# One stage of a hybrid sequence model: the S5 mixer by chunks of four tokens instead of token by token

## Chip, cores, metric

One core of a Trainium2 chip. The metric is the device time of one execution in microseconds; before the change three runs gave 3873.88, 3874.48 and 3877.62 us, a median of 3874.48 us.

## What is computed

A two-layer step over 256 prompt tokens and 8 samples of 4 tokens (288 tokens, width 2048): RMS norm, S5 mixer, a retrieval feed-forward over 16384 experts (PEER), then norm, RG-LRU mixer, PEER, final norm. The change touches the S5 mixer alone. Its reference, cut:

```python
bu_re = einsum("btgc,gpc->btgp", u, bb_re); bu_im = einsum("btgc,gpc->btgp", u, bb_im)   # 128 groups of 16 channels, 64 states
# the samples add a * h0 to their first token
s_re, s_im = scan over t of  s[t] = a * s[t-1] + bu[t]        # a complex, one per group and state
y = einsum("btgp,gcp->btgc", s_re, c_re) - einsum("btgp,gcp->btgc", s_im, c_im) + d_skip * h
y = gelu(y); out = y * sigmoid(y @ w_glu + b_glu)
```

The 128 x 64 = 8192 complex states are laid out as 64 columns ("state columns") of 128 partitions; four state columns belong to one tile of 128 channels, 16 tiles in all. The last states are outputs too.

## The kernel before, in words

Five engine programs run side by side and meet at semaphores; the order of the work is written out by hand. Line numbers are those of the profile.

Start: SyncE loads X (three tiles of 128 tokens, L321), then the S5 matrices B and C of a tile (L327, L333) and after them the first four GLU weight slabs (L344). VectorE and ScalarE work out the discrete parameters (L1373 to L1406, L1006 to L1015). The norm gives HN (L961, L963, L1342), TensorE turns it (L635), ScalarE copies it to HT (L978): channels on partitions, tokens along the free dimension.

S5 stage, 16 tiles: the complex recurrence is made real by rotation. In a tile of four state columns, TensorE multiplies B with the inputs (L735, L737), VectorE rotates 4 x 256 values by -phase * t with sine and cosine tables (L1425 to L1431), runs eight real scans of 256 tokens with the decay as factor (L1435), and rotates back by four products (L1441 to L1444). TensorE multiplies with C and D (L748, L754), ScalarE applies GELU into YT (L1036). The tables are made by ScalarE (L1021, L1022, sines at L1028 and L1032) with one VectorE step between (L1411). GpSimd scales B (L426 to L432), runs the samples' four steps one by one (L446 to L458) and writes the diagonal of D (L415).

After the stage, TensorE waits for all GELUs and makes the GLU product from YT (L648, 16 weight slabs of 1 MB, ring W of four slots), ScalarE the sigmoid (L1107), VectorE the gate (L1468). Then come the transposes back to token rows (L664), the second norm, the queries (L688) and, from about 620 us to the end, PEER and the LRU chain. None of that is changed, save that the gain row of the second norm is loaded later.

Two helpers matter for reading the code: `settle(ins)` on VectorE waits until its own last instruction has finished, `x.wait_ge(sem, n)` holds everything behind it on that engine.

## Time and profile before

| what | value |
|---|---|
| span of the profiled execution | 3880.3 us |
| time of the profiled execution | 3882.19 us |
| median of the three runs | 3874.48 us |
| busy: TensorE, VectorE, ScalarE, GpSimd | 59%, 75%, 12%, 38% of the span |
| chain that ended last | DMA 51%, DVE 26%, PE 16%, issue 6% |
| HBM traffic | 1404.75 MB, mean 362 GB/s |

Busy shares are means over stages with different limits: the PEER stages move expert rows at 410 to 428 GB/s, while the S5 stage, the first eleventh of the span, moves almost nothing. PE is a matmul, PEld its weight load, DVE is VectorE, ACT ScalarE, POOL GpSimd, SP SyncE. PEclk is the granted TensorE clock as a share of 2.4 GHz, 0.5 being 1.2 GHz. In a timeline row of several instructions the length runs from the first start to the last end; from one row's start to the next one's is what an instruction costs when the engine has work lined up (its "step"), and it is shorter than the listed duration, since the end of one overlaps the next.

### The profile page before, as it was taken

How to read it: one execution, taken by the hardware profiler on the slowest of the kernel's cores; microseconds unless marked ns; L12 is line 12 of the kernel's file. 1: busy time of each engine (PE TensorE's matmuls, PEld its weight loads, DVE VectorE, ACT ScalarE, POOL GpSimd, SP SyncE). 2: the span in 40 equal slices, each digit the busy share in tenths (PEclk: the TensorE clock that was granted, in tenths of full speed). 3: DMA queues.
4: the chain of work that ended last, by engine and by line, in shares of the span. 5: the costliest groups of instructions: out<-in, count | busy, mean ns of one | idle time of the engine just before them, and what ended most of it. 6: DMA issues, size and time to landing. Idle time of an engine off the chain costs nothing.

```text
span 3880.3 us, 30905 instructions
## 1 busy us (share of the span) xinstructions
PE 2277.3 (59%) x9698; PEld 1387.9 (36%) x9698; DVE 2899.6 (75%) x4162; ACT 456.3 (12%) x901; POOL 1471.3 (38%) x1739
## 2 busy tenths in 40 slices
PE   5667996000087777659499876470189773003776
PEld 2334775000022227559275346460056321001222
DVE  7995048999966568896768777868958768998655
ACT  6662121000000002220000012200000000000000
POOL 4885005434343333222323342223433434334332
PEclk8878998555599999779799988795599997556999
DMA  1002336999999999999999999999999999999998
GB/s 75 16 13 85 139 121 250 378 422 399 427 427 427 427 427 425 426 421 426 405 413 411 381 427 425 426 426 427 428 426 409 406 427 427 427 427 427 427 427 347
DMA packets 197425, 1404.75 MB, mean 362 GB/s; under 512 B 21952, under 2 KB 26304, under 8 KB 26768
## 3 DMA queue, kind: packets, MB, share of 16 engines
q0 software_dynamic: 167008, 1215.18, 74.8%
q1 hardware_dynamic: 30000, 187.74, 12.0%
q8 instruction: 73, 1.20, 0.1%
q14 instruction: 56, 0.46, 0.0%
q10 hardware_dynamic: 288, 0.18, 0.0%
HBM read 1399.77 MB, written 3.24 MB: 362 GB/s over the span
## 4 chain that ended last, share of the span: by engine, by line
DMA 51%; DVE 26%; PE 16%; issue 6%; ACT 1%; POOL 1%; POOLq 0%; DVEq 0%; ACTq 0%
DMA arena<-in_u_dram,ixs 27%; DMA arena<-in_v_dram,ixs 23%; DVE arena L1591 12%; PE ps L923 6%; PE ps L648 3%; PE ps L688 2%; PE ps L821 2%; DVE arena L1435 2%; DVE ps L1611 1%; POOL arena L496 1%; DVE HN L1442 1%; DVE HN L1443 1%; DVE HN L1444 1%; DVE arena L1431 1%; DVE arena L1430 1%
## 5 line engine op out<-in xcount | busy, mean ns | idle before, releaser
L923 PE MATMUL ps<-arena 128*128 128x512 f32 x2304 | 1115.4, 617 | 1200.7 <-DVE arena L1601 1003.2
L1591 DVE CUSTOM_DVE_ANT_0 arena<-arena,ps 128x2048 f32<-128x2048 f32 x556 | 1256.9, 2285 | 196.3 <-DMA arena<-in_u_dram,ixs 177.2
L923 PEld LDWEIGHTS ps<-arena 128*128 128x128 f32 x2304 | 409.0, 193 | 1877.1 <-issue 1362.6
L1611 DVE SCALAR_TENSOR_TENSOR ps<-arena,ps 128x1024 f32<-128x1024 f32 x564 | 726.7, 1288 | 434.2 <-DMA arena<-in_v_dram,ixs 434.2
L496 POOL DMA_INDIRECT arena<-in_u_dram,ixs x560 | 546.6, 976 | 1066.8 <-DVE arena L1591 998.7
L496 POOL DMA_INDIRECT arena<-in_v_dram,ixs x576 | 555.5, 964 | 949.0 <-PE ps L923 803.8
L821 PE MATMUL ps<-HT,W 128*128 128x160 f32 (+1 forms) x3072 | 407.0, 295 | 73.2 <-ACT HN L1207 30.0
L821 PEld LDWEIGHTS ps<-HT,W 128*128 128x128 f32 x3072 | 401.3, 197 | 93.9 <-issue 77.7
L1601 DVE TENSOR_SCALAR arena<-ident,arena 128x128 f32<-128x128 f32 x576 | 164.4, 285 | 60.3 <-PE ps L923 56.1
L849 PE MATMUL ps<-W,arena 128*128 128x128 f32 x1024 | 124.8, 283 | 42.9 <-DVE arena L1716 16.8
L849 PEld LDWEIGHTS ps<-W,arena 128*128 128x128 f32 x1024 | 121.1, 198 | 45.4 <-DVE arena L1716 17.0
L688 PE MATMUL ps<-HT,W 128*128 128x288 f32 x512 | 127.5, 411 | 0.0
L648 PE MATMUL ps<-arena,W 128*128 128x288 f32 x512 | 124.4, 406 | 0.7 <-ACT arena L1040 0.7
L961 ACT ACTIVATE HN<-X 128x2048 f32<-128x2048 f32 x15 | 28.5, 1902 | 771.2 <-DVE X L1619 758.9
L688 PEld LDWEIGHTS ps<-HT,W 128*128 128x128 f32 x512 | 98.1, 193 | 27.8 <-issue 1.0
L648 PEld LDWEIGHTS ps<-arena,W 128*128 128x128 f32 x512 | 97.2, 190 | 27.5 <-issue 0.8
L833 PE MATMUL ps<-HN,W 128*128 128x160 f32 (+1 forms) x256 | 51.8, 371 | 93.8 <-ACT HN L1219 91.9
L1468 DVE TENSOR_TENSOR arena<-arena 128x288 f32 x16 | 7.3, 458 | 127.4 <-ACT arena L1107 127.4
L754 PE MATMUL ps<-HN,arena 128*32 128x256 f32 x512 | 100.6, 479 | 0.0
L1435 DVE TENSOR_TENSOR_SCAN arena<-arena 128x256 f32<-128x256 f32 x128 | 85.5, 736 | 0.5
L833 PEld LDWEIGHTS ps<-HN,W 128*128 128x128 f32 x256 | 47.1, 259 | 97.8 <-ACT HN L1219 94.3
L748 PE MATMUL ps<-HT,arena 128*128 128x256 f32 x32 | 19.0, 696 | 99.7 <-DVE HN L1444 99.7
(252 smaller groups left out, 2136.6 us busy)
## 6 DMA issues: line engine op xcount, KB each, us to landing
W<-in_slabs_dram SPq DMA_DIRECT2D x168, 1024.0 KB, 10.1
arena<-in_u_dram,ixs POOLq DMA_INDIRECT x576, 16.5
arena<-in_v_dram,ixs POOLq DMA_INDIRECT x576, 16.7
GB<-in_norms_dram POOLq DMA_DIRECT2D x4, 1024.0 KB, 6.2
arena<-in_s_bc_dram SPq DMA_DIRECT2D x32, 128.0 KB, 2.2
X<-in_x_dram SPq DMA_DIRECT2D x3, 1024.0 KB, 10.9
out_y_dram<-HN SPq DMA_DIRECT2D x2, 1024.0 KB, 6.8
arena<-in_keys_dram POOLq DMA_DIRECT2D x1, 1024.0 KB, 5.1
```

The costliest lines, as they stand in the source:

```text
L496: pool.indirect_dma_start(ring[:, r, :], None, table, bass.IndirectOffsetOnAxis(ap=ixs[:, side, r:r + 1], axis=0)).then_inc(row_in[r], 16)
L648: mm = nc.tensor.matmul(ps[:, r % 2, 0:NT], W[:, slot, P * k:P * (k + 1)], rhs[:, k, :], start=(k == 0), stop=(k == KT - 1))
L688: mm = nc.tensor.matmul(ps[:, r % 2, 0:NT], W[:, slot, P * k:P * (k + 1)], HT[:, k, :], start=(k == 0), stop=(k == KT - 1))
L754: mm = nc.tensor.matmul(ps[rows, 5, 0:SEQ], c, PR[n][:, q, :], start=False, stop=(n == 3), skip_group_check=True)
L821: mm = nc.tensor.matmul(ps[:, bank, 0:CHAIN_COLS[c]], W[:, slot, P * k:P * (k + 1)], HT1[c][:, k, :], start=(k == 0), stop=(k == KT - 1))
L833: mm = nc.tensor.matmul(ps[:, bank, 0:CHAIN_COLS[c]], W[:, slot, at:at + P], XC[c][g % 2][:, 2 * (b // 4) + e, :], start=(e == 0), stop=(e ...
L849: mm = nc.tensor.matmul(ps[:, bank, out], Y[:, k, :], W[:, slot, P * k:P * (k + 1)], start=(k == 0), stop=(k == KT - 1))
L923: mm = nc.tensor.matmul(ps[:, 8 - SHARE + b, :], DG[(first + n) % DIAGS], ring[:, r, OWN + BANK * b:OWN + BANK * (b + 1)], start=(n == 0), ...
L1435: ins = V.tensor_tensor_scan(dst[:, q, :], dec[:, k * QK + q:k * QK + q + 1].to_broadcast([P, SEQ]), src[:, q, :], 0.0, ALU.mult, ALU.add)
L1591: V.tensor_tensor_reduce(ring[:, r, :], ring[:, r, :], token, 1.0, 0.0, ALU.mult, ALU.add, AV[:, COL_AT[t] + n:COL_AT[t] + n + 1]).then_in ...
L1601: V.tensor_scalar(DG[v % DIAGS], ident[:], weight, None, ALU.mult).then_inc(diag_set, 1)
L1611: V.scalar_tensor_tensor(to, row, weight, total, ALU.mult, ALU.add).then_inc(row_used[r], 1)
```

## The change

The 256 prompt tokens become 64 chunks of four, the 8 samples 8 more: 72 columns. Two channel tiles (eight state columns) are one pair; there are 8 pairs.

- The input is normalised in a new layout: SyncE loads x again as 72 partitions x 4 tokens into the weight ring W (12 DMAs), ScalarE squares it (4 of 2048), VectorE scales it (4 of 2048). The former norm with its transposes goes; X is still loaded for the residual.
- Per pair VectorE builds two sets of matrices: inputs times a^(3-s) and C times a^(s+1), 16 products or differences of 512 elements (`scaled`, 8 each).
- TensorE turns the first set (16 transposes in four groups, each copied out by ScalarE), multiplies it with C to get the matrix from a token to a later token of its chunk (`s5_kernel`, 24 small matmuls), which ScalarE copies in seven pieces into a block triangular matrix TOEP; it turns the chunks' inputs (8 transposes in two groups).
- `s5_inputs`: 16 matmuls of 72 columns give what each chunk adds to its state. `states`: rotation, two scans of 512 elements (eight state columns of 64 chunks in one, the factor being 0 at each start), rotation back; the sample's end state is two small adds.
- `s5_outputs`: per state column one matmul with TOEP and two with the second set on the state before the chunk; 24 of 72 columns. GELU in 16 instructions of 144 elements that put the tokens back in order.
- GpSimd makes the phase products (`phases`, before ScalarE), the samples' start states (`start_states`), the diagonals and, once, the samples' end term (`sample_ends`).
- On SyncE the GLU slabs 0 and 1 are loaded once the norm has freed W, 2 and 3 after the last pair's outputs.

The diff, cut to the new code (what it replaces stands above; three dots mark what is left out):

```diff
+LC = 4
+CHUNKS = NT // LC
+PCH = SEQ // LC
+S5_PAIRS = KT // 2
+PQ = 2 * QK
...
+            def s5_bc_pair(n):
+                if n >= 2:
+                    sp.wait_ge(s5_bcc, n - 1)
+                    sp.wait_ge(s5_k, n - 1)
+                for e in range(2):
+                    sp.dma_start(BCS[:, n % 2, :, e, :], s5_bc[2 * n + e].rearrange("p (a n) -> p a n", a=4)
+                                 ).then_inc(s5_bc_in[n % 2], 16)
+            s5_bc_pair(0)
+            sp.dma_start(S0[:].rearrange("p c q b -> p (c q b)"), s5_h0).then_inc(s5_h0_in, 16)
+            s5_bc_pair(1)
...
+            sp.wait_ge(chunk_norm, LC)
+            for r in range(2):
+                sp.dma_start(W[:, r, :], slabs[r]).then_inc(slab_in[r], 16)
+            for n in range(2, S5_PAIRS):
+                s5_bc_pair(n)
...
+            def phases(n):
+                qs = slice(PQ * n, PQ * (n + 1))
+                if n > 0:
+                    pool.wait_ge(s5_tab, n)
+                nc.gpsimd.tensor_tensor(PRD, iota[:, 0:PCH].unsqueeze(1).to_broadcast([P, PQ, PCH]),
+                                        phi4[:, qs].unsqueeze(2).to_broadcast([P, PQ, PCH]), ALU.mult).then_inc(s5_ph, 1)
+            def start_states(n):
+                if n >= 2:
+                    pool.wait_ge(s5_y, n - 1)
+                nc.gpsimd.tensor_copy(SP[n % 2][:, :, :, PCH:CHUNKS], S0[:, :, PQ * n:PQ * (n + 1), :]).then_inc(s5_h, 1)
...
+            sample_ends()
+            pool.wait_ge(chunk_norm, LC)
+            start_states(0)
+            start_states(1)
+            phases(1)
+            for n in range(2, S5_PAIRS):
+                diagonals(n)
+                start_states(n)
+                phases(n)
+            pool.wait_ge(s5_s, S5_PAIRS)
...
+            def s5_turned(n, g):
+                e, c = g // 2, g % 2
+                pe.wait_ge(s5_ab, n + 1)
+                if g > 0:
+                    pe.wait_ge(s5_btc, LC * n + g)
+                elif n > 0:
+                    pe.wait_ge(s5_utc, 2 * n)
+                for q in range(QK):
+                    mm = nc.tensor.transpose(ps[:, 4, P * q:P * (q + 1)], IMX[:, c, QK * e + q].rearrange("p s n -> p (s n)"),
+                                             ident[:])
+                mm.then_inc(s5_bt, 1)
...
+            def s5_kernel(n):
+                pe.wait_ge(s5_dd, n + 1)
+                pe.wait_ge(s5_bc_in[n % 2], 32 * (n // 2 + 1))
+                if n > 0:
+                    pe.wait_ge(s5_kc, n)
+                for q in range(PQ):
+                    e, rows, out = q // QK, slice(QC * (q % QK), QC * (q % QK + 1)), slice(QC * q, QC * (q + 1))
+                    for c in range(2):
+                        nc.tensor.matmul(ps[:, 5, out], IMX[:, c, q].rearrange("p s n -> p (s n)"), BCS[:, n % 2, 2 + c, e, rows],
+                                         start=(c == 0), stop=False, skip_group_check=True)
+                    mm = nc.tensor.matmul(ps[P - QC:P, 5, out], ident[:, rows], DD[:, (2 * n + e) % 4, rows],
+                                          start=False, stop=True, skip_group_check=True)
+                mm.then_inc(s5_k, 1)
...
+            def s5_prepare(n):
+                s5_turned(n, 0)
+                s5_kernel(n)
+                for g in range(1, 4):
+                    s5_turned(n, g)
+                if n == 0:
+                    pe.wait_ge(chunk_norm, LC)
+                s5_chunks(2 * n)
+                s5_chunks(2 * n + 1)
...
+            def s5_inputs(n):
+                pe.wait_ge(s5_btc, LC * (n + 1))
+                pe.wait_ge(s5_utc, 2 * (n + 1))
+                if n > 0:
+                    pe.wait_ge(s5_bur, n)
                 for c in range(2):
+                    for q in range(PQ):
+                        at = CHUNKS * (q % QK)
+                        mm = nc.tensor.matmul(ps[:, 2 * c + q // QK, at:at + CHUNKS], ABT[:, c, q, :], U4[:, PQ * n + q, :],
+                                              start=True, stop=True)
                 mm.then_inc(s5_bu, 1)
...
+            def s5_outputs(n):
+                pe.wait_ge(s5_kc, n + 1)
+                pe.wait_ge(s5_ca, n + 1)
+                pe.wait_ge(s5_h, n + 1)
+                pe.wait_ge(s5_s, n + 1)
+                if n > 0:
+                    pe.wait_ge(s5_yg, n)
+                for q in range(PQ):
+                    at = CHUNKS * (q % QK)
+                    out = ps[:, 6 + q // QK, at:at + CHUNKS]
+                    nc.tensor.matmul(out, TOEP[:, n % 2, q, :], U4[:, PQ * n + q, :], start=True, stop=False, skip_group_check=True)
+                    for c in range(2):
+                        mm = nc.tensor.matmul(out, OMX[:, c, q].rearrange("p s n -> p (s n)"), SP[n % 2][:, c, q, :],
+                                              start=False, stop=(c == 1), skip_group_check=True)
                 mm.then_inc(s5_y, 1)
+            pe.wait_ge(consts, 2)
+            s5_prepare(0)
+            s5_inputs(0)
+            for n in range(S5_PAIRS):
+                if n + 1 < S5_PAIRS:
+                    s5_prepare(n + 1)
+                    s5_inputs(n + 1)
+                s5_outputs(n)
...
+            def tables(n):
+                act.wait_ge(s5_f, n + 1)
+                if n >= 2:
+                    act.wait_ge(s5_s, n - 1)
+                A(SIN[n % 2], PRD, ACT.Sin, scale=-TWO_PI_LOW).then_inc(astep, 1)
                 act.wait_ge(astep, ast.next())
                 A(PRD, PRD, ACT.Abs).then_inc(astep, 1)
                 act.wait_ge(astep, ast.next())
+                A(COS[n % 2], PRD, ACT.Sin, scale=-TWO_PI_LOW, bias=cst[:, 0:1]).then_inc(s5_tab, 1)
...
+            def prepare(n):
+                for g in range(4):
+                    e, c = g // 2, g % 2
+                    act.wait_ge(s5_bt, 4 * n + g + 1)
+                    if n > 0:
+                        act.wait_ge(s5_bu, n)
+                    A(ABT[:, c, QK * e:QK * (e + 1), :], ps[:, 4, :].rearrange("p (q n) -> p q n", q=QK), ACT.Copy
+                      ).then_inc(s5_btc, 1)
+                    if g == 0:
+                        kernels(n)
+                for k in (2 * n, 2 * n + 1):
+                    act.wait_ge(s5_ut, k + 1)
+                    A(U4[:, QK * k:QK * (k + 1), :], ps[:, 4, 0:QK * CHUNKS].rearrange("p (q j) -> p q j", q=QK), ACT.Copy
+                      ).then_inc(s5_utc, 1)
+            def kernels(n):
+                act.wait_ge(s5_k, n + 1)
+                act.wait_ge(s5_pad, 1)
+                if n >= 2:
+                    act.wait_ge(s5_y, n - 1)
+                for out in range(LC - 1, -1, -1):
+                    cols = slice(QC * out, QC * (out + 1))
+                    lag = LC - 1 - out
...
+                ins.then_inc(s5_kc, 1)
+            def gelu_y(n):
+                act.wait_ge(s5_y, n + 1)
+                for s in range(LC):
+                    for q in range(QK):
+                        src = ps[QC * s:QC * (s + 1), 6:8, CHUNKS * q:CHUNKS * (q + 1)]
+                        dst = YT[QC * q:QC * (q + 1), 2 * n:2 * n + 2, :].rearrange("p k (j s) -> p k j s", s=LC)[:, :, :, s]
+                        ins = A(dst, src, ACT.Gelu)
+                ins.then_inc(s5_yg, 1)
...
+            for n in range(S5_PAIRS):
+                if n + 1 < S5_PAIRS:
+                    decays(n + 1)
+                    tables(n + 1)
+                    prepare(n + 1)
+                if n + 2 < S5_PAIRS:
+                    compact(n + 2)
+                gelu_y(n)
...
+            V.memset(IMX[:].rearrange("p c q s n -> p (c q s n)"), 0.0)
+            V.memset(OMX[:].rearrange("p c q s n -> p (c q s n)"), 0.0).then_inc(vstep, 1)
...
+            def fractions(n):
+                dve.wait_ge(s5_ph, n + 1)
+                plus = T[0].rearrange("p (q j) -> p q j", q=PQ)
+                settle(V.tensor_scalar(plus, PRD, ROUND, None, ALU.add))
                 V.scalar_tensor_tensor(PRD, plus, ROUND, PRD, ALU.subtract, ALU.subtract).then_inc(s5_f, 1)
+                dve.wait_ge(s5_f, n + 1)
+            def scaled(to, n, first, tables):
+                qs, cube4 = slice(PQ * n, PQ * (n + 1)), [P, PQ, LC, 16]
+                re, im, neg = (w[:, :, qs].rearrange("p s q -> p q s").unsqueeze(3).to_broadcast(cube4) for w in tables)
+                a, b = (BCC[:, n % 2, first + c].unsqueeze(2).to_broadcast(cube4) for c in range(2))
+                t = [w.rearrange("p (q s n) -> p q s n", q=PQ, s=LC) for w in T]
+                V.tensor_tensor(t[0], a, re, ALU.mult)
+                V.tensor_tensor(t[1], b, im, ALU.mult)
+                V.tensor_tensor(t[2], a, neg, ALU.mult)
+                settle(V.tensor_tensor(t[3], b, re, ALU.mult))
+                for c in range(2):
+                    for h in range(2):
+                        rows = slice(64 * h, 64 * (h + 1))
+                        ins = V.tensor_tensor(to[rows, c, :, :, 16 * h:16 * (h + 1)], t[2 * c][rows], t[2 * c + 1][rows],
+                                              ALU.subtract)
+                return ins
+            def input_matrices(n):
+                dve.wait_ge(s5_bcc, n + 1)
+                if n > 0:
+                    dve.wait_ge(s5_bt, 4 * n)
+                    dve.wait_ge(s5_k, n)
+                scaled(IMX, n, 0, (GFR, GFI, GFN)).then_inc(s5_ab, 1)
+                dve.wait_ge(s5_ab, n + 1)
...
+                V.tensor_tensor(tile(M[0]), re[:, :, :, prompt], tile(cos), ALU.mult)
+                V.tensor_tensor(tile(M[1]), im[:, :, :, prompt], tile(sin), ALU.mult)
+                V.tensor_tensor(tile(M[2]), im[:, :, :, prompt], tile(cos), ALU.mult)
+                V.tensor_tensor(tile(M[3]), re[:, :, :, prompt], tile(sin), ALU.mult)
...
+                V.tensor_tensor_scan(flat[1], flat[4], flat[0], 0.0, ALU.mult, ALU.add)
+                settle(V.tensor_tensor_scan(flat[3], flat[4], flat[2], 0.0, ALU.mult, ALU.add))
+                p0, p1, p2, p3 = M[0], M[2], *(w.rearrange("p (q j) -> p q j", q=PQ) for w in T[0:2])
+                V.tensor_tensor(p0, cos, M[1], ALU.mult)
+                V.tensor_tensor(p1, sin, M[3], ALU.mult)
+                V.tensor_tensor(p2, sin, M[1], ALU.mult)
+                settle(V.tensor_tensor(p3, cos, M[3], ALU.mult))
+                if n >= 2:
+                    dve.wait_ge(s5_y, n - 1)
+                last, now = slice(PCH - 1, PCH), SP[n % 2]
+                for c, (a, b, op) in enumerate(((p0, p1, ALU.add), (p2, p3, ALU.subtract))):
+                    V.tensor_tensor(now[:, c, :, 1:PCH], a[:, :, 0:PCH - 1], b[:, :, 0:PCH - 1], op)
+                    ins = V.tensor_tensor(SF[:, c, qs].unsqueeze(2), a[:, :, last], b[:, :, last], op)
+                ins.then_inc(s5_s, 1)
+                dve.wait_ge(s5_s, n + 1)
...
+            for s in range(LC):
+                V.scalar_tensor_tensor(xn[:, :, s, :], W[0:CHUNKS, s, :].rearrange("p (q n) -> p q n", q=S5_Q), inv[:, s:s + 1],
+                                       GB[0:CHUNKS, 0, :].rearrange("p (q n) -> p q n", q=S5_Q), ALU.mult, ALU.mult
+                                       ).then_inc(chunk_norm, 1)
...
+            for n in range(S5_PAIRS):
+                if n + 1 < S5_PAIRS:
+                    fractions(n + 1)
+                    input_matrices(n + 1)
+                output_matrices(n)
+                states(n)
```

## Rows read from the trace of the kernel before

**Rows 1.** The windows view, three stages: us, busy per engine (count), PEclk, DMA share, GB/s.
```profile
0.00:42.00 42.00, 14.09 (x54) 10.01 (x55) 15.86 (x38) 32.32 (x57) 12.56 (x38) 1.00 0.42 164
42.00:355.00 313.00, 200.59 (x1017) 97.37 (x1015) 301.51 (x335) 181.05 (x315) 253.35 (x368) 0.80 0.08 26
355.00:482.00 127.00, 125.59 (x548) 98.13 (x548) 6.88 (x15) 13.72 (x22) 0.00 (x0) 1.00 0.35 124
```

**Rows 2.** The chain in order of time, the change-over to the GLU product: start, us, what.
```profile
348.95 5.98 PE ps L754 x32
356.83 124.44 PE ps L648 x512
```

**Rows 3.** Groups by line and form, start to 800 us: busy us, mean ns.
```profile
L1435 DVE TENSOR_TENSOR_SCAN arena<-arena 128x256 f32<-128x256 f32 x128 | 85.5, 736 | 0.5
...
L1425 DVE TENSOR_TENSOR arena<-ps,arena 128x1024 f32<-128x1024 f32 x16 | 19.4, 1213 | 2.4 <-PE ps L737 2.4
```

**Rows 4.** Timeline of VectorE in the first LRU chain: start us, us, what.
```profile
1582.25 1.44 DVE L1701 TENSOR_TENSOR_SCAN HN<-HN 128x128 f32<-128x128 f32 x4
...
1585.74 0.68 DVE L1716 TENSOR_TENSOR arena<-arena,HN 128x512 f32<-128x512 f32 x1
1586.34 0.68 DVE L1719 TENSOR_TENSOR HN<-arena,HN 128x512 f32<-128x512 f32 x1
```

**Rows 5.** Timeline of the first microseconds, VectorE.
```profile
2.09 1.02 DVE L1373 MEMSET arena<- 128x1152 f32 x1 [2.09 <-issue]
...
9.56 0.23 DVE L1403 TENSOR_TENSOR arena<-arena 128x64 f32<-128x64 f32 x1
9.71 0.22 DVE L1404 TENSOR_TENSOR arena<-arena 128x64 f32<-128x64 f32 x1
9.96 0.22 DVE L1405 TENSOR_TENSOR arena<-arena 128x64 f32<-128x64 f32 x1
...
17.66 2.35 DVE L1342 SCALAR_TENSOR_TENSOR HN<-X,nrm,GB 128x2048 f32<-128x2048 f32 x1
```

**Rows 6.** Timelines of ScalarE: the norm stage, the S5 stage, then the LRU chain.
```profile
30.84 1.07 ACT L978 ACTIVATE HT<-ps 128x512 f32<-128x512 f32 x2
...
311.92 1.28 ACT L1028 ACT_TABLE_LOAD   x1 [4.57 <-DVE arena L1411]
...
1480.51 0.28 ACT L1202 ACTIVATE HN<-ps 128x128 f32<-128x128 f32 x1 [6.74 <-PE ps L821]
1480.68 0.17 ACT L1205 ACTIVATE arena<-ps 128x3 f32<-128x3 f32 x1
...
1698.33 0.68 ACT L1219 ACTIVATE HN<-ps,CH 128x160 f32<-128x160 f32 x2 [12.38 <-DVE HN L1719]
```

**Rows 7.** Timelines of TensorE, with one ScalarE row that answers to the first.
```profile
31.47 4.29 PE L635 MATMUL ps<-ident,HN 128*128 128x128 f32 x24 [1.39 <-ACT HT L978]
32.62 0.60 ACT L978 ACTIVATE HT<-ps 128x512 f32<-128x512 f32 x1 [0.71 <-PE ps L635]
...
494.56 5.09 PE L635 MATMUL ps<-ident,HN 128*128 128x128 f32 x24
...
1517.19 17.62 PE L821 MATMUL ps<-HT,W 128*128 128x160 f32 x128
...
1569.82 10.92 PE L821 MATMUL ps<-HT,W 128*128 128x160 f32 x64 [25.09 <-ACT HN L1207]
...
1745.99 3.74 PE L849 MATMUL ps<-W,arena 128*128 128x128 f32 x32
```

**Rows 8.** Windows view: two short stretches, columns as in the first group.
```profile
494.00:500.00 6.00, 5.51 (x28) 4.47 (x26) 3.91 (x5) 3.55 (x6) 1.06 (x2) 0.61 0.47 165
8.00:10.00 2.00, 0.00 (x0) 0.00 (x0) 1.86 (x12) 0.00 (x0) 0.00 (x0) 1.00 1.03 434
```

**Rows 9.** Groups of GpSimd by line and form, whole span.
```profile
L426 POOL TENSOR_TENSOR arena<-arena 128x128 f32<-128x128 f32 x64 | 29.4, 489 | 0.2 <-POOL arena L432 0.2
...
L558 POOL TENSOR_TENSOR arena<-arena 128x512 f32<-128x512 f32 x16 | 20.0, 1269 | 49.4 <-ACT arena L1134 49.4
```

More of the change, by code:

```diff
@@ L385, in _ @@
             st = Steps()
[L386 to L387 removed]
+            pool.dma_start(GB[:, 0, :], norms[0:1, :].partition_broadcast(P)).then_inc(gain_in, 16)
             nc.gpsimd.memset(ident[:], 0.0).then_inc(pstep, 1)
@@ new lines, in _ @@
+            settle(V.tensor_scalar(t1, phi[:, 0:64], 4.0, None, ALU.mult))
+            settle(V.tensor_scalar(t2, t1, ROUND, ROUND, ALU.add, ALU.subtract))
+            V.tensor_tensor(phi4, t1, t2, ALU.subtract)
+            V.tensor_copy(PWR[:, 0, :], abr)
+            settle(V.tensor_copy(PWI[:, 0, :], abi))
+            tmp = [w.rearrange("p (s q) -> p s q", q=64) for w in T[0:2]]
+            times([PWR[:, 1, :], PWI[:, 1, :]], [abr, abi], [abr, abi], [w[:, 0, :] for w in tmp])
+            square = [w[:, 1:2, :].to_broadcast([P, 2, 64]) for w in (PWR, PWI)]
@@ new lines, in _ @@
+            fractions(0)
+            input_matrices(0)
+            dve.wait_ge(chunk_sq, LC)
+            V.tensor_scalar(var, sums, 1.0 / D, EPS, ALU.mult, ALU.add).then_inc(chunk_var, 1)
+            dve.wait_ge(chunk_root, 1)
+            settle(V.reciprocal(inv, root))
+            dve.wait_ge(gain_in, 16)
+            xn = XN[0:CHUNKS].rearrange("p (q s n) -> p q s n", q=S5_Q, s=LC)
+            for s in range(LC):
+                V.scalar_tensor_tensor(xn[:, :, s, :], W[0:CHUNKS, s, :].rearrange("p (q n) -> p q n", q=S5_Q), inv[:, s:s + 1],
+                                       GB[0:CHUNKS, 0, :].rearrange("p (q n) -> p q n", q=S5_Q), ALU.mult, ALU.mult
+                                       ).then_inc(chunk_norm, 1)
@@ new lines, in _ @@
+            dve.wait_ge(chunk_norm, LC)
+            for h in range(2):
+                V.memset(DEC[h][:, :, 0:1], 0.0)
+                for c in range(2):
+                    ins = V.memset(SP[h][:, c, :, 0:1], 0.0)
+            settle(ins)
+            for n in range(S5_PAIRS):
[4 more added lines that the diff above has]
+                states(n)
+            dve.wait_ge(s5_y, S5_PAIRS)
@@ L1464, in _ @@
+            dve.wait_ge(s5_yg, S5_PAIRS)
             with dve.Fori(0, 4) as g:
```

456 lines of the change are left out of this document (163 added, 293 removed).

## The prediction, made before the changed kernel ran

> **What bounds it now.** I read the windows by stage first [rows 1]: from 42 to 355 us VectorE is busy 301.5 of 313 us, ScalarE 181, TensorE 201, and DMA hardly at all. So the S5 stage is VectorE's, 19.6 us a tile, 39.1 us a pair of tiles. The chain in order of time says the same and shows the change-over [rows 2]: the last C products (L754) end at 354.9 and the GLU product starts at 356.8, after the last GELU. Everything behind 356.8 is the same code, so what the stage gains or loses before that point moves the end one for one. In the groups by line [rows 3] the eight scans of 256 cost 0.74 us each as listed, the rotations of 1024 elements 1.21. The change shortens both by four, so VectorE will surely win; the question is who is late next.
>
> **Prices.** VectorE: two 512-element products follow each other after 0.60 us (1585.74 to 1586.34), four scans of 128 take 1.44 us, a step of 0.34; with 256 at 0.67 that is linear, so a scan of 512 is 1.31 us [rows 3, 4]. A 64-element operation steps by 0.15, and by 0.25 where it has a `settle` behind it; a fill runs at 0.89 ns an element; the norm's 2048 elements take 2.35, in a row some 2.2 [rows 5]. ScalarE, copying from PSUM: 512 elements 0.60 with a step of 0.48, 128 with 0.17, so 256 with 0.27; a table load is 1.28; a sigmoid of 160 steps by 0.29 [rows 6]. TensorE: from the first of four transposes to the start of their copy is 1.15 us; 24 transposes in a row take 5.09 (0.21 each), 32 matmuls of 128 columns 3.74 (0.11 each) [rows 7]. The first of these two stood at a mean clock share of 0.61 [rows 8], near the 1.2 GHz level, the second agrees with 2.4. GpSimd: 128 elements 0.49, 512 elements 1.27 [rows 9].
>
> No row has a matmul of 72 columns with its own 128x128 weights. Below, it can't beat the 0.11 of the weight load beside it at the high level; above, a low-level load (0.21) not hidden by so short a matmul, plus the matmul: about 0.55. I take 0.22 at the low level, as the transposes are nearest in shape (a load and a short stream each).
>
> The Trainium skill (TensorE: Matmul & The Clock Gate, section LDWEIGHTS) gives the load as columns over 1.2 GHz, 107 ns for 128 whatever the level; the 0.11 rows agree, the 0.21 row does not, and there the measurement decides. By that rule the 40 dense matmuls of a pair would take 4.5 us instead of 8.8.
>
> **The loop of one pair.** I follow it from Z, the end of the previous `s5_outputs`. What I found decisive is GpSimd: `phases(n+1)` stands behind `start_states(n+1)`, which waits for Z, and VectorE's first step of the round, `fractions(n+1)`, waits for `phases(n+1)`. So VectorE stands idle during the 24 output matmuls and the whole preparation of the next pair starts only after them.
> 1. GpSimd: copy 0.4, phases 1.27, hand-overs 0.1: Z+1.8.
> 2. VectorE: `fractions` 2 x 0.6 + 0.1; `input_matrices` 8 x 0.60 + 2 x 0.12 (halves of 64 partitions are no shorter): Z+8.2. The access by runs of 16 and broadcast is taken to be free.
> 3. TensorE, low level: four transposes 1.15, `s5_kernel` 16 x 0.22 and 8 with only 32 weight columns at 0.15: Z+14.1.
> 4. ScalarE: seven copies of 256, 2.0, and the second group's copy 0.6: Z+16.7.
> 5. Transposes and copy in turn through one PSUM bank: 2 x (1.15 + 0.6) and 2 x (1.15 + 0.4): Z+23.3.
> 6. `s5_inputs` 16 x 0.22, `s5_outputs` 24 x 0.22, hand-overs 0.4: Z+32.5.
>
> Beside it: ScalarE's GELUs (load 1.28, 16 at 0.17 to 0.29 [rows 6], I take 0.19), the decays 0.6 and tables (load, three of 512) 3.3 end at Z+8.2 to Z+9.8, where the copy of group 0 is due at 9.3: hidden, but with no slack. VectorE's `output_matrices` (5.05) and `states` (4 x 0.60, ends 0.3, 2 x 0.60, scans 2.6, 4 x 0.60, 2 x 0.7, four `settle`: 10.9) end at Z+24.1, before the inputs product does. The matrices' loads (512 KB a pair) and the compaction (1.3) are covered by the output matmuls; without that cover they would add 1.3.
>
> At the high level throughout: 8.2 + 0.6 + 2.4, copies 2.6, turns 4.4, inputs 1.8 end at Z+20; then `states` is the last at 24.1, and the outputs 2.7 give 27.0. After a 25 us idle 64 matmuls of 160 columns took 10.92 where 128 took 17.62 [rows 7], so 2.1 were lost before the clock rose. TensorE idles 8 us of every round. I expect the low level through the preparation and a rise within the outputs: **31.5 us a pair**, against 39.1.
>
> **Before the loop.** VectorE's fills grow from 1.0 to 3.6 us, some 40 more small operations cost 7.5: parameters ready at 19.6 instead of 10.4 [rows 5]. `fractions`, `input_matrices(0)`: 26. Meanwhile 3.4 MB arrive at 434 GB/s in 8 us [rows 8], the squares end near 23. Root with table 2.1, four norm steps 2.2 each: 37.3. Then decays 0.6, the copies, turns and inputs of pair 0 (steps 4 to 6): 51.5; of pair 1 with its transposes and kernel: 70.5; outputs(0): 75.5. The twelve chunk loads issue under this; dropped are the three norm tiles.
>
> **After it.** Last pair from Z: `output_matrices` 5.05, `states` 10.9, outputs 5.3, GELUs 3.1, hand-overs 0.3: 24.7. Then the GLU product begins on an idle TensorE, 2.1 lost. Slabs 2 and 3 are issued at the last outputs and needed 15.5 us after the start: hidden. The second gain row is read 130 us later: hidden.
>
> **Sum.** 75.5 + 6 x 31.5 + 24.7 + 2.1 = 291.3, against 356.8: 65.5 gained. Profiled execution: 3882.2 (span 3880.3) becomes 3816.7. It stood 7.7 above the median of the runs, so the median becomes **3809 us**.
>
> **Rivals.**
> - High level (or low-level loads at 0.11): 27.0 a pair; outputs(0) 4 earlier, the tail 3.5 shorter in all. Gain 65.5 + 27 + 7.5 = 100: 3775. For it: in the stage before, the mean share was 0.80 [rows 1]. Against: there TensorE was two thirds busy with long matmuls. The load rule of the Trainium skill (TensorE: Matmul & The Clock Gate, LDWEIGHTS) lies here. 0.15.
> - Dearer small steps: 72-column matmuls at 0.3, GELUs at 0.29 and small-run accesses 10% slower add 64 x 0.08 + 0.5 + 1.0 = 6 a pair, nearly 9 outside the loop: gain 20, 3854. For it: ScalarE's sigmoid step of 0.29 and VectorE's 0.67 scan step show that the short prices vary by form; no row denies it. 0.18.
> - Slower: the weight load is not hidden behind 72 columns, 0.55 each at the low level. 56 such matmuls are on the path of a pair: 56 x 0.33 = 18.5, six times 111, and 96 outside: 32. 143 - 65.5 makes it 77 slower, 3952. It turns to a loss from 0.37 a matmul. Against it stand the 24 transposes at 0.21, load included. 0.03.
> - The path isn't shortened at all, because some wait I read as covered adds 8 us a pair: within 0.2%, 3874. 0.02.
>
> The forecast has 0.62. The range, 3775 to 3852, takes in the high-level case and nearly the dear one. 0.2% (8 us) is about what a measurement of this kernel can tell from no change; only the last two cases and the far tail of the dear one lie outside "faster": 0.95 faster, 0.02 the same, 0.03 slower.
>
> **What would show it.** Right: GLU product starting near 290; VectorE busy near 23 of 31.5 us a pair, its longest idle before `fractions`, released by GpSimd; the seven copies starting when the kernel matmuls end; clock share 0.5 to 0.65 in the stage; four transposes and a copy some 1.75 apart. Wrong: VectorE without gaps (then 27 or less), a listed step of 72-column matmuls over 0.3, a GELU group over 6 us, or the GLU product halting for slab 2.

## The result: slower, with the profile after

The changed kernel took 3931.86 us, the median of four runs (3930.53 to 3933.73), against 3875.51 before: 1.0144 times, 95% interval 1.013 to 1.0159. The forecast was 3809, range 3775 to 3852. The profiled execution has a span of 3928.9 us, 48.6 more than before.

The windows of the changed kernel by stage, with the columns of [rows 1]:

```profile
0.00:42.00 42.00, 7.26 (x36) 6.64 (x36) 36.70 (x82) 18.81 (x26) 18.88 (x31) 1.00 0.73 198
42.00:355.00 313.00, 225.44 (x1046) 204.71 (x1045) 157.15 (x260) 126.52 (x251) 14.64 (x27) 1.00 0.05 17
355.00:482.00 127.00, 102.22 (x426) 85.34 (x427) 19.24 (x34) 22.42 (x47) 1.71 (x3) 1.00 0.27 96
```

VectorE's work did fall as meant, from 301.5 of 313 us to 157.2 in the same window. TensorE's rose, and it is now the busiest. The chain that ended last gives the change-over:

```profile
409.06 127.00 PE ps L647 x512
```

The GLU product starts at 409.06 and not at 356.8 as in [rows 2]: the stage is 52.2 us longer. The product itself took 127.00 instead of 124.44. Together that is 54.8 us; the medians differ by 56.4. The spans of the two profiled executions differ by less, 48.6: the execution before lay 6.7 us above the median of its kernel, and the missing 6.2 us lie behind the GLU product, in code that is the same.

Groups by line and form, start to 410 us (busy us, mean ns, idle before):

```profile
L795 PE MATMUL ps<-W,arena 128*128 128x72 f32 x256 | 67.9, 421 | 0.0
L741 PE MATMUL ps<-HN,arena 128*128 128x32 f32 x256 | 66.8, 401 | 0.0
L778 PE MATMUL ps<-HT,arena 128*128 128x72 f32 x256 | 56.6, 422 | 4.4 <-issue 3.8 <-ACT HT L1082 0.6
L1109 ACT ACTIVATE arena<-ps 32x144 f32<-32x144 f32 x128 | 53.5, 418 | 127.4 <-PE ps L795 126.0
L728 PE MATMUL ps<-ident,arena 128*128 128x128 f32 x128 | 35.1, 430 | 109.7 <-DVE arena L1492 83.8 <-ACT arena L1076 25.9
...
L1475 DVE TENSOR_SCALAR arena<-arena 128x512 f32<-128x512 f32 x8 | 4.1, 507 | 146.5 <-POOL arena L441 146.4
```

Here the error can be counted. Line 778 is `s5_inputs`: 16 matmuls a pair, 128 in all, and the trace has 256 rows of it. The 128 transposes of L728 have 128 rows. So a float32 matmul is two passes, each with its own weight load, and a transpose is one. The busy rows of a pass (one load and one stream through the array) say 421 ns, but they overlap; what a pass costs is the step from one start to the next, in the timeline of one round:

```profile
237.62 6.89 ACT L1109 ACTIVATE arena<-ps 32x144 f32<-32x144 f32 x16 [15.00 <-PE ps L795]
237.65 0.29 POOL L448 COPY W<-GB 128x128 f32<-128x128 f32 x1 [43.75 <-PE ps L795]
237.90 1.04 POOL L441 TENSOR_TENSOR arena<-iota,HN 128x512 f32<-128x512 f32 x1
239.05 0.53 DVE L1475 TENSOR_SCALAR arena<-arena 128x512 f32<-128x512 f32 x1 [23.40 <-POOL arena L441]
240.42 0.69 DVE L1485 TENSOR_TENSOR arena<-arena,HN 128x512 f32<-128x512 f32 x1
245.79 1.11 PE L728 MATMUL ps<-ident,arena 128*128 128x128 f32 x4 [8.21 <-DVE arena L1492]
246.70 0.90 PE L741 MATMUL ps<-HN,arena 128*128 128x32 f32 x4
247.77 1.06 PE L741 MATMUL ps<-HN,arena 128*128 128x32 f32 x4
249.01 1.06 PE L741 MATMUL ps<-HN,arena 128*128 128x32 f32 x4
...
256.56 2.71 ACT L1099 ACTIVATE arena<-ps 128x256 f32<-128x256 f32 x7 [7.42 <-PE ps L743]
259.30 0.60 ACT L1076 ACTIVATE arena<-ps 128x512 f32<-128x512 f32 x1
260.04 1.09 PE L728 MATMUL ps<-ident,arena 128*128 128x128 f32 x4 [2.46 <-ACT arena L1076]
```

And from the chain, the end of that round:

```profile
266.20 7.07 PE ps L778 x32
273.70 0.85 PE ps L795 x4
274.98 0.85 PE ps L795 x4
```

The order is the one the prediction described: outputs end (237.6), GpSimd, `fractions` after 23.4 us of idle VectorE, input matrices, transposes, `s5_kernel`, copies, turns, inputs. But a state column of `s5_kernel` is 1.24 us (247.77 to 249.01), the inputs 7.07 for 32 passes (a step of 0.21), a state column of the outputs 1.28 (273.70 to 274.98). The inputs products start 45.94 us apart (220.27, 266.20, 312.14), against 31.5 forecast and 39.1 before.

### The profile page after: what moved, and what is told of

Same layout as the page of the kernel before. It is cut to its first block, busy times and chain, and to the rows that moved or that the text cites. A ratio compares the mean times of both kernels' runs of the same rounds, so it can differ in the third digit from the quotient of the medians.

```text
span 3928.9 us, 30658 instructions
## 1 busy us (share of the span) xinstructions
PE 2325.1 (59%) x9810; PEld 1518.8 (39%) x9810; DVE 2792.0 (71%) x4156; ACT 402.9 (10%) x841; POOL 1239.5 (32%) x1394
## 3 DMA queue, kind: packets, MB, share of 16 engines
q1 hardware_dynamic: 34288, 190.10, 12.2%
## 4 chain that ended last, share of the span: by engine, by line
DMA 51%; PE 21%; DVE 20%; issue 5%; ACT 2%; POOL 1%; POOLq 0%; SPq 0%; DVEq 0%; ACTq 0%
DMA arena<-in_u_dram,ixs 27%; DMA arena<-in_v_dram,ixs 24%; DVE arena L1711 12%; PE ps L947 6%; PE ps L647 3%; PE ps L687 2%; PE ps L845 2%; PE ps L778 1%; PE ps L795 1%; PE ps L741 1%; DVE ps L1731 1%; PE ps L793 1%; PE ps L728 1%; POOL arena L495 1%; DVE arena L1492 0%
## 5 line engine op out<-in xcount | busy, mean ns | idle before, releaser
L845 PE MATMUL ps<-HT,W 128*128 128x160 f32 (+1 forms) x3072 | 403.6, 293 | 77.0 <-ACT arena L1240 33.9
L728 PE MATMUL ps<-ident,arena 128*128 128x128 f32 x128 | 35.1, 430 | 109.7 <-DVE arena L1492 83.8
```

What stands on the lines that cost most here:

```text
L728: mm = nc.tensor.transpose(ps[:, 4, P * q:P * (q + 1)], IMX[:, c, QK * e + q].rearrange("p s n -> p (s n)"), ident[:])
L845: mm = nc.tensor.matmul(ps[:, bank, 0:CHAIN_COLS[c]], W[:, slot, P * k:P * (k + 1)], HT1[c][:, k, :], start=(k == 0), stop=(k == KT - 1))
```

## The experiments

The tables give the medians; "to changed" is the difference from 3931.86, "round" the distance of two inputs products in the middle of the stage, "GLU" the start of the GLU product (409.06 in the changed kernel). Each ratio is to runs of the kernel before made beside that experiment, whose medians were 3876.36 to 3877.14 and not 3875.51. "To changed" has no such partner, so a difference under 2 us, as that of e10, says nothing by itself; there the GLU product's start is read.

| run | median us | to changed | ratio to before (95%) | round | GLU |
|---|---|---|---|---|---|
| e1_phases_first | 3886.10 | -45.8 | 1.0026 (1.0015 to 1.0036) | 38.4 | 364.5 |
| e2_kernel_twice | 3987.23 | +55.4 | 1.028 (1.0263 to 1.0297) | 52.8 | 464.1 |
| e3_wide | 3888.84 | -43.0 | 1.0027 (1.0017 to 1.0038) | 41.0 | 368.5 |
| e4_fill_gap | 3921.07 | -10.8 | 1.0111 (1.0094 to 1.0128) | 44.1 | 398.3 |
| e5_first_wide | 3844.55 | -87.3 | 0.9918 (0.9901 to 0.9934) | 32.4 to 34.0 | 322.5 |
| e6_all_four | 3803.57 | -128.3 | 0.9809 (0.9792 to 0.9825) | 27.3 | 281.1 |
| e7_gelu_twice | 3939.75 | +7.9 | 1.016 (1.0143 to 1.0177) | 45.95 | 416.1 |
| e8_products_thrice | 3936.06 | +4.2 | 1.0149 (1.0132 to 1.0166) | 45.95 | 413.3 |
| e9_copies_late | 3919.65 | -12.2 | 1.0104 (1.0089 to 1.012) | 44.25 | 396.4 |
| e10_ends_later | 3930.30 | -1.6 | 1.0131 (1.0116 to 1.0147) | 45.95 | 408.05 |
| e11_order_only | 3867.47 | -64.4 | 0.997 (0.9958 to 0.9982) | 35.8 | 345.95 |
| e12_all_five | 3802.46 | -129.4 | 0.9801 (0.9788 to 0.9814) | 27.3 | 280.9 |
| e13_squares_first | 3925.08 | -6.8 | 1.0128 (1.0113 to 1.0144) | 45.95 | 404.2 |
| e14_all_six | 3799.97 | -131.9 | 0.9803 (0.979 to 0.9817) | 27.3 | 276.9 |

### What sets the round

**e1_phases_first**

```diff
-                start_states(n)
                 phases(n)
+                start_states(n)
...
             pool.wait_ge(stores, 32)
+            pool.wait_ge(s5_h, S5_PAIRS)
```

> Edit: on GpSimd the phase products of pair n+1 are issued ahead of the sample states' copy that waits for the previous outputs. Theory A (TensorE's passes in series set the round, plus the hole in which it waits for the input matrices): the input matrices are then ready when the outputs end, TensorE's idle time before its first group of transposes (about 8 us a round) goes, the round falls from 45.9 to about 38 us, and the time by 6 or 7 rounds of 7.7 to 8.2, so 46 to 57 us: 3875 to 3886. Rival B (ScalarE is as late as VectorE: GELUs, decays and tables end 10.95 us after the outputs and the first copy stands behind them): that copy was hidden behind the kernel matmuls (they end 11 us after the start of the group); if B holds, copies are late by a few us and the round stays at 42 or more, a gain below 30 us. Rival C (VectorE sets the round): no change.

The round fell by 7.5 us, the GLU product came 44.6 us earlier. In its timeline the transposes follow the outputs at once, while VectorE has no more hole before `fractions`:

```profile
214.31 1.06 PE L796 MATMUL ps<-W,arena 128*128 128x72 f32 x4
215.17 1.06 PE L729 MATMUL ps<-ident,arena 128*128 128x128 f32 x4
...
226.32 0.60 ACT L1077 ACTIVATE arena<-ps 128x512 f32<-128x512 f32 x1
```

Rival B doesn't hold: the first copy comes at 226.32, right behind the GELUs, decays and tables, and costs the path 0.9 us: the third group of transposes starts 15.1 us after the first, where it was 14.3 (245.79 to 260.04). ScalarE, which had been beside the path, now touches it.

**e2_kernel_twice**

```diff
-                    for c in range(2):
+                    for c in (0, 1, 0, 1):
```

The third matmul starts the sum anew, so nothing of the computation is changed after all.

> Edit: the 16 C matmuls of the kernel step are issued twice a pair into the same sums (this part of the computation comes out changed). Theory A (every one of these lies on the path, at two passes of 0.22 us): 16 x 0.44 = 7.1 us a round, over 7 rounds and the first pair 50 to 57 us: 3982 to 3989. Rival (one pass of 0.22 a matmul, as the prediction priced it): 25 to 28 us, 3957 to 3960. Rival B (ScalarE's GELUs and tables end just as the kernel does, and it is their lateness that counts): the same as A, since the copies come behind the kernel. Rival C (VectorE sets the round): below 5 us.

The round grew by 6.8 us, the GLU product came 55.0 us later, the time grew by 55.4. That is 16 times 0.43 us a round: two passes a matmul, all on the path. The rows of the line doubled with it, for 256 matmuls:

```profile
L741 PE MATMUL ps<-HN,arena 128*128 128x32 f32 x512 | 121.4, 401 | 0.0
```

 The prediction's single pass would have given 28.

**e7_gelu_twice** and **e8_products_thrice** load the two other engines. In the first the loop over the 16 GELUs runs twice, with a wait for itself between; in the second, three products of `output_matrices` run three times:

```diff
-                V.tensor_tensor(t[0], a, re, ALU.mult)
-                V.tensor_tensor(t[1], b, im, ALU.mult)
-                V.tensor_tensor(t[2], a, neg, ALU.mult)
+                for left in range(0 if first == 0 else 2, -1, -1):
+                    V.tensor_tensor(t[0], a, re, ALU.mult)
+                    V.tensor_tensor(t[1], b, im, ALU.mult)
+                    ins = V.tensor_tensor(t[2], a, neg, ALU.mult)
+                    if left:
+                        settle(ins)
```

> Edit: the 16 GELUs of a pair are done twice. Theory A (6.9 more us on ScalarE lie beside the hole and the kernel matmuls; the first copy is hidden up to about 8 us of lateness): nothing in the rounds, only 6.9 behind the last pair: 3936 to 3942. Rival B (ScalarE sets the round, the GELU at 0.43 and not at 0.19 us is what failed): 7 to 8 times 6.9, 3980 to 3990.

> Edit: three of the four products of the output matrices are done three times, 3.8 us more VectorE work a pair. Theory A (the new states are there 11 us before the outputs may start, so VectorE has room): nothing in the rounds, 3.8 behind the last pair at most: 3932 to 3937. Rival C (VectorE sets the round): 8 times 3.8, 3960 to 3965.

Neither moved the round by more than 0.01 us. Both paid once, behind the last pair: the GLU product came 7.0 and 4.2 us later. In the changed kernel ScalarE's GELUs and VectorE's output matrices are beside the path in every round but the last. ScalarE had no more room than that: of the 7.4 us for which it waited before the seven copies, 0.5 was left in e7. Its copies are another matter:

**e9_copies_late**

```diff
                       ).then_inc(s5_btc, 1)
-                    if g == 0:
-                        kernels(n)
                 for k in (2 * n, 2 * n + 1):
...
                       ).then_inc(s5_utc, 1)
+                kernels(n)
```

> Edit: on ScalarE alone, the seven kernel copies stand behind the other turns of a pair and not between the first and the second. Theory A (they hold the one bank through which the matrices are turned, so they are on the path of TensorE): 2.7 to 2.8 us a round less, 43.1 a round, 8 pairs: 19 to 23 us, 3909 to 3913. Rival (the copies are beside other work, or their time comes back because the outputs then wait for them): 3928 to 3935.

1.7 us a round, not 2.8. I had taken all 2.7 us of the copies for path; but the second group's transposes (1.1 us) run beside them in the changed kernel, from 256.45, and only the rest is saved.

### What the passes cost, and the clock

**e3_wide**

```diff
-                        mm = nc.tensor.matmul(ps[:, 2 * c + q // QK, at:at + CHUNKS], ABT[:, c, q, :], U4[:, PQ * n + q, :],
-                                              start=True, stop=True)
+                        two = min(2, PQ - q)
+                        mm = nc.tensor.matmul(ps[:, 2 * c + q // QK, at:at + two * CHUNKS], ABT[:, c, q, :],
+                                              U4[:, PQ * n + q:PQ * n + q + two, :], start=True, stop=True)
```

and the same in `s5_outputs`. The second 72 columns are written over by the next state column, whose first matmul starts a new sum. The expectation speaks of sums that change in the outputs product; with that start they don't.

> Edit: the matmuls of the inputs and outputs products stream 144 columns in place of 72 with the same weights (the second 72 are overwritten by the next matmul, in the outputs product they add up with it and change the result). Theory A1 (each pass is bound by its weight load of 0.22 us at the low clock level): 80 passes a round hardly longer, below 1.5 us a round, 0 to 10 us in all: 3932 to 3942. Theory A2 (the streaming counts beside the load): 72 more columns at 1.2 GHz are 0.06 us a pass, 4.8 us a round, 35 to 38 us in all: 3967 to 3970. Theory A3 (a longer stream brings the clock to the high level): passes near 0.12 us, the round some 8 us shorter, 3870 to 3880.

Twice the columns made the kernel 43 us faster. Windows over the inputs and the outputs of one round, then the outputs of the next round in the timeline:

```profile
202.00:208.40 6.40, 6.37 (x32) 6.40 (x33) 0.00 (x0) 2.35 (x3) 0.00 (x0) 0.60 0.00 0
208.40:214.30 5.90, 5.90 (x51) 5.85 (x49) 0.00 (x0) 0.00 (x0) 0.00 (x0) 1.00 0.00 0
```

```profile
249.69 0.65 PE L798 MATMUL ps<-W,arena 128*128 128x144 f32 x4
250.18 0.41 PE L795 MATMUL ps<-HT,arena 128*128 128x144 f32 x2
250.42 0.65 PE L798 MATMUL ps<-W,arena 128*128 128x144 f32 x4
```

A state column of the outputs takes 0.74 us in place of 1.28, 0.123 a pass. The clock record now changes: 0.60 of full speed over the inputs, 1.00 over the outputs, and the latter are dense passes of 0.123. A round saves 4.9 us, where A3 said 8: the kernel matmuls and turns stay at the low level. In the changed kernel the same products, as dense but 72 columns wide, took 17.3 us without a pause, and their passes did not get shorter.

The wider stream alone is no gift. While the level was still low its passes started 0.24 us apart (202.41, 202.65, 202.89), those of 72 columns in the changed kernel 0.21 (220.74, 220.95, 221.16). And at the high level the eighth state column, whose matmuls keep their 72 columns, took 0.62 us for six passes and not 0.74. From e5 below:

```profile
190.91 0.34 PE L796 MATMUL ps<-HT,arena 128*128 128x72 f32 x2
191.08 0.61 PE L799 MATMUL ps<-W,arena 128*128 128x72 f32 x4
191.53 0.60 PE L729 MATMUL ps<-ident,arena 128*128 128x128 f32 x4
```

So the gain is the clock's, and the 43 us are what is left of it after the dearer stream.

**e4_fill_gap**

```diff
+                if n + 2 < S5_PAIRS:
+                    fill(18)
```

> Edit: behind each outputs product TensorE does 18 matmuls of 256 columns whose result nobody reads, in the hole of about 8 us in which it waits for the input matrices. Theory A1 (low level stays; 18 times 2 passes of 0.21 us are 7.7 us): hidden or nearly, 0 to 10 us slower: 3932 to 3942. Theory A3 (the hole is what keeps the clock down: filled, the passes after it run at the high level): the transposes and the kernel matmuls near 0.12 us a pass, the round 8 to 15 us shorter, 3830 to 3880. Rival: the fillers themselves are dearer than the hole (0.43 us a pass): 7 x 7.7 = 54 us slower, 3986.

Neither theory's number. Windows over the outputs (72 columns), then over the kernel matmuls behind the fillers, and three rows of their timeline:

```profile
222.00:231.60 9.60, 9.60 (x47) 9.60 (x46) 0.00 (x0) 0.00 (x0) 0.00 (x0) 0.50 0.00 0
241.60:246.30 4.70, 4.70 (x40) 4.21 (x39) 4.59 (x8) 1.92 (x3) 0.00 (x0) 0.98 0.00 0
246.50:249.00 2.50, 2.50 (x14) 2.24 (x13) 2.46 (x7) 0.00 (x0) 0.00 (x0) 0.50 0.00 0
```

```profile
244.92 0.63 PE L746 MATMUL ps<-HN,arena 128*128 128x32 f32 x4
245.66 0.65 PE L746 MATMUL ps<-HN,arena 128*128 128x32 f32 x4
...
247.73 1.06 PE L746 MATMUL ps<-HN,arena 128*128 128x32 f32 x4
```

Over the 72-column outputs the record says 0.50. It rose while the fillers ran (0.98 behind them); the kernel's state columns up to 245.66 took 0.74 us each, then the clock fell to 0.50 while the narrow matmuls ran without a pause, and the column took 1.24 again. That settles how the changed kernel's record is to be read. There the same column takes 1.24 us while the clock column says 1.00. Nor does the column show the rise at the start of the changed kernel's GLU product, where twice as many rows begin in a microsecond a little later:

```profile
410.00:413.00 3.00, 3.00 (x7) 2.03 (x7) 0.00 (x0) 0.00 (x0) 0.00 (x0) 1.00 0.00 0
416.00:420.00 4.00, 4.00 (x19) 3.11 (x18) 0.00 (x0) 0.23 (x1) 0.00 (x0) 1.00 0.00 0
```

So a 1.00 from the start of a trace says nothing until another value has been read. By its durations the whole stage ran at 1.2 GHz. The fillers themselves ended 1.8 us after the hole, so only 1.9 us a round was left.

The Trainium skill (TensorE: Matmul & The Clock Gate, section LDWEIGHTS) gives one formula for the weight load in ns, its columns over 1.2, and names no clock level; for 128 columns that is an estimate of 107 ns. At the high level the passes lie near it (0.103 with 72 columns, 0.123 with 144); at the low level one of 72 columns took 0.21 us, twice that, and there the measurement decides. The Trainium skill (FP8 and Floating Point Precision, section TensorE Precision Notes) also counts four passes for true float32; this trace has two rows of load and two of matmul for each, and no run here looks inside a row.

**e5_first_wide** has the edits of e1 and e3 together; **e11_order_only** has three changes of order (e1's, e9's and the one below) without the wider streams; **e6_all_four** has the three and the wider streams. The new order on ScalarE is

```diff
+            decays(1)
+            tables(1)
             for n in range(S5_PAIRS):
                 if n + 1 < S5_PAIRS:
-                    decays(n + 1)
-                    tables(n + 1)
                     prepare(n + 1)
                 if n + 2 < S5_PAIRS:
                     compact(n + 2)
+                    decays(n + 2)
+                    tables(n + 2)
                 gelu_y(n)
```

> Edit: the two earlier edits together: phase products first on GpSimd, and 144 columns in the inputs and outputs matmuls. Theory A (passes in series on TensorE, and their length is the clock's): the hole of 7.6 us and the 4.9 us of the shorter passes are different pieces of the round, so they add: 45.9 - 7.5 - 4.9 = 33.5 us a round, 88 us below the changed kernel: 3841 to 3850, faster than the kernel before by 0.6 to 0.9%. With TensorE without a hole the clock may stay high through the transposes and the kernel matmuls (0.745 in place of 1.24 us a state column): up to 4.5 us a round less, 3815. Rival B (ScalarE, whose GELUs, decays and tables end 10.9 us after the outputs, is next): nothing beyond 33.5, since the first copy can't come earlier. Rival (both edits work by the same thing, the filled hole): no more than the better one, 3886.

> Edit: the three changes of order together (phases first, tables ahead of the GELUs, copies behind the turns), without the longer streams. Theory A (at the low level the passes stay 0.22 us): 38.4 - 2.8 - up to 1 us of what was late behind the GELUs = 34.6 to 35.6 a round, 3860 to 3868. Theory A3 (a TensorE with few holes comes to the high level without longer streams too): 27 to 30 a round, 3803 to 3825.

> Edit: as the one before, and on ScalarE the decays and tables of the pair after the next stand before the GELUs (in the 15 us in which it waits for the outputs), and the seven kernel copies behind the turns. Theory A (TensorE's chain sets the round): the 2.7 us of the copies and what was late behind the GELUs go, 29 to 30 us a round at the clock mix of the kernel before this; at the high level all through, transposes 0.6, kernel 6.0, three turns 4.5, two chunk turns 2.2, inputs 3.9, outputs 5.9, hand-overs 0.5: 23.6, but VectorE needs 22.7 busy: 24 to 26. Time 3790 to 3830. Rival B' (VectorE becomes the bound at once, by its chain rotation, scan, rotation after the inputs): 30 us or more, 3830 or above. Rival (ScalarE was never in the way): as the kernel before this.

The two edits of e5 add up (45.8 + 43.0 = 88.8; measured 87.3). Order alone, with TensorE busy 32.5 of 36.0 us (187 to 223 us), leaves the passes at 0.21 (the inputs still took 7.07 us) and gives 35.8 a round; order and wider streams give 27.3. Closing the holes alone left the passes where they were; with the longer streams in the same order they shortened. From e6, one round's marks:

```profile
184.04 5.71 PE L780 MATMUL ps<-HT,arena 128*128 128x144 f32 x32 [0.55 <-issue]
195.41 0.60 PE L729 MATMUL ps<-ident,arena 128*128 128x128 f32 x4
200.18 0.63 PE L742 MATMUL ps<-HN,arena 128*128 128x32 f32 x4
...
203.30 1.09 PE L729 MATMUL ps<-ident,arena 128*128 128x128 f32 x4 [1.17 <-ACT arena L1080]
```

The kernel matmuls are at the high level too, except the last; the first copy is late by 1.2 us behind the GELUs. This version beats the kernel before by 1.9%.

### Before the loop

**e10_ends_later** moves GpSimd's `sample_ends()` behind the wait for the norm; **e13_squares_first** moves, beyond that, `compact(0)` behind the second of ScalarE's four squares.

> Edit: on GpSimd alone, the samples' end term is computed after the norm and not beside the first input matrices. Theory A (the products of the first input matrices took 1.5 us each and not 0.6, and the four sums 5.3 and not 2.8, because GpSimd's operations on the same memory ran at the same time): the first input matrices are ready at 29 us and not at 34.6, the norm ends near 39 and not at 44.4, 5 to 5.5 us less: 3926 to 3927. Rival (another reason, the layout of the data of the first pair): no change, 3932.

> Edit: as the version with the samples' end term later, and on ScalarE two of the four squares of the norm stand ahead of the first compaction, which waits for the matrices of the first pair. Theory A (in the version before it the first input matrices were ready at 30.3 us, but the squares ended at 32.4 because the first stood behind that wait): the squares end near 28.5, the norm starts at about 30.7 and ends at 39.9, and not at 43.4; inputs(0) start at 50.7. 3.5 us less than that version, 5.1 less than the changed kernel: 3926 to 3927.5. Rival (the rows of the input land as late as the matrices, so the order makes no difference): 3930.

Timelines of VectorE, first in the changed kernel, then in e10:

```profile
23.93 0.69 DVE L1485 TENSOR_TENSOR arena<-arena,HN 128x512 f32<-128x512 f32 x1 [1.02 <-ACT arena L1047]
24.54 1.57 DVE L1486 TENSOR_TENSOR arena<-arena,HN 128x512 f32<-128x512 f32 x1
26.03 1.56 DVE L1487 TENSOR_TENSOR arena<-arena,HN 128x512 f32<-128x512 f32 x1
29.30 5.30 DVE L1492 TENSOR_TENSOR arena<-arena 64x512 f32<-64x512 f32 x4
```

```profile
25.49 0.68 DVE L1486 TENSOR_TENSOR arena<-arena,HN 128x512 f32<-128x512 f32 x1
26.09 0.68 DVE L1487 TENSOR_TENSOR arena<-arena,HN 128x512 f32<-128x512 f32 x1
27.41 2.79 DVE L1492 TENSOR_TENSOR arena<-arena 64x512 f32<-64x512 f32 x4
32.59 0.17 DVE L1559 TENSOR_SCALAR HN<-HN 72x4 f32<-72x4 f32 x1 [2.39 <-ACT arena L1115]
```

Without GpSimd beside it a product costs 0.6 us and not 1.5, and the input matrices are ready at 30.3, not 34.6. But the norm gained 1.0 us only: VectorE now waited 2.4 us for the squares, which stood on ScalarE behind the compaction's wait for the first matrices. These landed at 23.51, and at 22.56 in the changed kernel, so by an estimate the gain would have been near 2 us had they come as early. My expectation had left that second wait out. e13 took it away: its norm starts at 30.36 and the GLU product 4.9 us earlier than in the changed kernel, 5.1 expected; its median, 6.8 lower, agrees within its spread (3924.06 to 3930.42).

**e12_all_five** and **e14_all_six** put e10 and then e13 on top of e6.

> Edit: the version with phases first, the tables ahead, the copies late, 144 columns, and the samples' end term after the norm. Theory A: the 5 us of the norm's start come off the 3803.6 of the version with four edits: 3797 to 3800, faster than the kernel before by 1.9 to 2.1%. Rival (the norm is not on the path, or the end term now delays the first states): 3803.

> Edit: the version with five edits, and the squares ahead of the first compaction. Theory A: the GLU product starts at 277.5 and not at 280.9: 3799. Rival (inputs(0) is not what sets the first outputs): 3802.5.

e12 gained 0.2 us at the GLU product against e6, so the rival of its expectation was right (3803; 3802.46 measured) and not theory A: moving the end term is worth nothing while the squares stand behind the compaction. e14 gained 4.2, as its theory A has it. The medians of e6, e12 and e14 lie too close, for the spread of their runs, to rank them by; each stands at 0.98 of the kernel before.

## Why the prediction was wrong, point by point

| part | forecast | measured | where it went |
|---|---|---|---|
| until outputs(0) end | 75.5 | 99.8 | norm 7.1; kernels, inputs, outputs 17.2 |
| six rounds | 189 | 275.4 | 14.4 a round |
| last pair, GLU's start | 24.7 | 33.9 | outputs 5.2, GELUs 3.7 |

These are 119.9 us more than forecast (99.8 is 82.46, the start of the inputs product of pair 1, plus the 17.3 us that inputs and outputs take). The 2.1 us put down for the GLU product on an idle TensorE were 2.6. The median lies 122.9 above the forecast; the cause of the 2.5 that are left stays open, and single executions spread as much.

- **The failed step is the price of a matmul, steps 3 and 6.** "0.22 at the low level, as the transposes are nearest in shape" took one row for one matmul. Per round: kernel step 10.8 us against 5.9 (with the transposes), inputs and outputs 17.3 against 9.2. That is 13.0 of the 14.4 us a round. In its place the runs showed two passes a matmul, 0.43 us at the low level (e2). The eight matmuls with 32 weight columns, put at 0.15, were two passes as well, 0.39: 1.9 of the 13.0. The rows of before could have told: the GLU product is 16 slabs times 16, 256 matmuls, and [rows 2] has 512. "32 matmuls of 128 columns 3.74 (0.11 each)" from [rows 7] was the same misreading; they were 16. The transpose is the one operation that has a row apiece, and I had taken it for the pattern.
- **The rise of the clock within the outputs** (1.0 us a round) did not come. In e3 and e4 the level rose in the loop, over 144-column products and fillers of 256; over the 72-column outputs of e4 the record stayed at 0.50. What the chip looks at was not measured. The high-level rival's 27.0 us a pair, met by e6's 27.3, is a coincidence of sizes: e6 needed the new order and the wider streams for it, and had double passes but not the waits of the old order.
- **The slower rival had the threshold, not the mechanism**: it turned to a loss from 0.37 us a matmul, and a matmul took 0.43. But it put the price down to one weight load that isn't hidden, and the trace has two loads and two streams. Its formula gives 143 x 0.21 / 0.33 - 65.5 = 26 us slower; the matmuls of 32 weight columns (1.9 a pair), norm, GELUs and the clock account for most of the rest. The price was within the bounds of 0.11 to 0.55 that I gave, so a chance of 0.03 for its upper half had no support.
- **GpSimd's order** was read rightly: 8.2 us from the outputs' end to the transposes, forecast 8.2; e1 took it away, worth 45.8 us.
- **GELU** 0.43 us each, not 0.19: 6.9 us a pair, hidden in each round by the longer kernel step (e7) and paid once, 3.7.
- **The norm** ended at 44.4, not 37.3. "The squares end near 23" ignored their place in ScalarE's queue, and the products of the first input matrices were priced without GpSimd beside them (e10, e13).
- **Right**: fractions and input matrices 6.7 us (6.4), turns 6.3 (6.6), VectorE's slack, matrix loads and slabs hidden. The seven copies were put too short, 2.0 for 2.7.
- **Its own signs and sums**: two of the signs of being wrong came, a 72-column matmul over 0.3 us and a GELU group over 6 us. The dearer rival was added up short, 5.1 + 0.5 + 1.0 being 6.6 a pair and not 6, some 4 us in all.

## What to carry to other kernels

Before a row's duration is used as the price of an instruction, count the rows of a line against the instructions that the code issues: here a float32 matmul was two rows, each with a weight load, and a transpose one. A price whose bounds lie five to one apart and that is paid 56 times a round is the forecast; give its upper half a real chance. In a loop across engines look at what stands behind a wait in the program of each engine: moving one small copy behind the operation that others need was worth 46 us, and the same arithmetic went from 1.4% slower to 2% faster by order and stream width alone.

## What was not expected of the hardware

- With 144 columns streamed in place of 72 a pass came to 0.123 us and not 0.21, because the clock rose there; at one and the same level the wider pass is the dearer one (0.24 to 0.21, 0.123 to 0.103). Useless columns bought 43 us. Over matmuls of 32 columns, dense as they were, the clock fell again (0.98 to 0.50).
- A float32 matmul is two rows of load and two of stream, a float32 transpose one of each; the price on the path, 0.43 us at the low level, is that of both passes (e2).
- A clock column of 1.00 can mean "no change recorded yet" (e4 against the changed kernel, 1.24 us at 0.50 and at 1.00): durations at both levels have to be compared.
- VectorE's 512-element product took 1.5 us instead of 0.6 while GpSimd worked on 512-element operations of its own (e10), and GpSimd's took 1.5 to 1.6 instead of 1.1 to 1.3. The Trainium skill (GPSIMD Engine Reference, section Specifications) says that GpSimd's SBUF interfaces are shared with VectorE, and that the two contend when a VectorE instruction has two SBUF inputs, among other cases. These products have two, and the trace agrees.
